# The two compressors' first layer as plain fp32 products of raw weights, keys and values in two column halves

## The reference, cut to what matters

```python
def compress(z, pe, w1, w2):
    c = z.reshape(B, T // CMP_STRIDE, CMP_STRIDE, G, N)
    blk = jnp.concatenate([c[:, :-1], c[:, 1:]], axis=2) + pe[None, None, :, None, :]
    blk = blk.transpose(0, 3, 1, 2, 4).reshape(B, G, n_cmp, CMP_LEN * N)
    return jax.nn.gelu(blk @ w1) @ w2

k_cmp = compress(kc, pe_k, ck_w1, ck_w2)
v_cmp = compress(vc, pe_v, cv_w1, cv_w2)
```

## Time and profile before

| | |
|---|---|
| median of 3 runs | 970.83 us (970.83 to 971.23) |
| profiled execution | 971.14 us, of which span 969.3 us |
| TensorE busy | 949.5 us (98%), granted clock 0.999 |
| VectorE, ScalarE, GpSimd busy | 703.2, 422.5, 439.5 us |
| chain that ended last | TensorE 83%, VectorE 12% |
| `CLO` on GpSimd, `CHI` on ScalarE | eight each, median 2.41 and 1.06 us |

### The profile page before, as it was taken

How to read it: one execution, slowest core, us unless ns; L and a number is a source line. 1 busy time by engine, 2 the same in 40 slices (tenths; PEclk the granted TensorE clock), 3 DMA queues, 4 the chain that set the end, 5 groups by cost and what they waited for, 6 DMA issues and landing times.

```text
span 969.3 us, 20667 instructions
## 1 busy us (share of the span) xinstructions
PE 949.5 (98%) x8504; PEld 767.3 (79%) x8504; DVE 703.2 (73%) x1170; ACT 422.5 (44%) x846; POOL 439.5 (45%) x473
## 2 busy tenths in 40 slices
PE   7999999999999999999999999999999999999997
PEld 5788777777777777776777888888999888888886
DVE  3799797565655966869777870489787774489987
ACT  4134341323313525546574454553444443345573
POOL 3367547335442865767665466445223225500000
PEclk9999999999999999999999999999999999999999
DMA  9344633212222648525336548043333433345452
GB/s 259 103 131 133 139 87 69 43 35 70 77 59 65 195 131 186 153 67 130 59 100 176 148 150 263 24 152 109 89 111 112 118 96 87 97 142 177 138 194 89
DMA packets 157365, 115.47 MB, mean 119 GB/s; under 512 B 21413, under 2 KB 139951, under 8 KB 157272
## 3 DMA queue, kind: packets, MB, share of 16 engines
q1 hardware_dynamic: 147820, 105.21, 37.8%
q10 hardware_dynamic: 9420, 8.95, 4.0%
q0 software_dynamic: 32, 0.00, 0.0%
HBM read 102.84 MB, written 11.30 MB: 118 GB/s over the span
## 4 chain that ended last, share of the span: by engine, by line
PE 83%; DVE 12%; issue 2%; ACT 1%; DMA 1%; POOL 0%; SPq 0%; DVEq 0%; ACTq 0%
PE ps L2424 32%; PE ps L2903 5%; PE ps L2902 5%; PE ps L2907 5%; PE ps L2544 3%; PE ps L2790 3%; PE ps L2963 2%; PE ps L2964 2%; PE ps L2965 2%; PE ps L2733 2%; PE ps L2940 2%; PE ps L2937 2%; PE ps L2936 2%; DVE XF L1517 2%; PE ps L2438 1%
## 5 line engine op out<-in xcount | busy, mean ns | idle before, releaser
L2424 PE MATMUL ps<-HHI,WHI 128*128 128x512 f32 x440 | 176.8, 402 | 0.7 <-DVE HLO L1549 0.7
L2424 PE MATMUL ps<-HLO,WHI 128*128 128x512 f32 x440 | 176.8, 402 | 0.0
L829 POOL TENSOR_TENSOR WLO<-WRAW,WHI 128x1024 fp32r<-128x1024 f32 (+1 forms) x51 | 103.2, 2026 | 102.1 <-ACT WHI L949 102.0
L930 POOL TENSOR_TENSOR WLO<-WRAW,WHI 128x512 fp32r<-128x512 f32 x50 | 72.5, 1457 | 118.6 <-ACT WHI L1317 117.2
L2424 PE MATMUL ps<-HHI,WLO 128*128 128x512 f32 x440 | 117.6, 397 | 0.0
L870 POOL TENSOR_TENSOR WLO<-WRAW,WHI 128x256 fp32r<-128x256 f32 x136 | 108.7, 802 | 14.4 <-ACT WHI L1166 7.0
L2424 PEld LDWEIGHTS ps<-HHI,WHI 128*128 128x128 f32 x440 | 82.6, 188 | 24.9 <-issue 7.5
L2424 PEld LDWEIGHTS ps<-HLO,WHI 128*128 128x128 f32 x440 | 82.6, 188 | 19.2 <-issue 1.6
L2424 PEld LDWEIGHTS ps<-HHI,WLO 128*128 128x128 f32 x440 | 80.7, 188 | 18.4 <-issue 1.4
L833 POOL CAST WHI<-WRAW 128x256 fp32r<-128x256 f32 (+1 forms) x93 | 46.7, 503 | 100.4 <-PE ps L2424 100.2
L2903 PE MATMUL ps<-HLO,WHI 128*128 128x512 f32 x200 | 77.9, 389 | 0.0
(11 more groups left out here) (512 smaller groups left out, 2316.1 us busy)
## 6 DMA issues: line engine op xcount, KB each, us to landing
WRAW<-in_w_in SPq DMA_DIRECT2D x47, 512.0 KB, 4.5
WRAW<-in_w_gate SPq DMA_DIRECT2D x22, 512.0 KB, 3.8
WRAW<-in_w_up SPq DMA_DIRECT2D x22, 512.0 KB, 3.8
WRAW<-in_w_down SPq DMA_DIRECT2D x19, 512.0 KB, 3.5
spilled<-SQ SPq DMA_DIRECT2D x24, 256.0 KB, 2.5
GATES<-spilled SPq DMA_DIRECT2D x6, 768.0 KB, 5.0
WRAW<-in_w_in SPq DMA_DIRECT2D x16, 256.0 KB, 3.5
WRAW<-in_w_branch SPq DMA_DIRECT2D x32, 128.0 KB, 2.9
```

The source lines that it names most:

```text
L829: return pool.tensor_tensor(lo[:, 0:chunks, :], WRAW[:, n % NRAW, 0:chunks, :], hi[:, 0:chunks, :].bitcast(F32), ALU.subtract)
L930: pool.tensor_tensor(lo, raw_half(item[1], item[2]), hi.bitcast(F32), ALU.subtract).then_inc(w_lo, 1)
L2424: last = pe.matmul(DB[g % 2][:, :], (wlo if which == "low" else whi)[:, c, :], lo if which == "x_low" else hi, start=a == 0, stop=a == 3 * ...
```

## The change

The eight `cmp` jobs leave the list. SP loads the raw weights of a part for keys and for values into two pairs of own buffers `CRAW` (`cmp_weights`); parts 0 and 1 are loaded ahead of the tiles rwkv 6 and rwkv 7, parts 2 and 3 ahead of rwkv 11 and rwkv 12, when the products of part 0 and of part 1 are done. TensorE multiplies `XF` by `CRAW` as they are, in plain fp32, in four packs of eight products (`compressed`) behind the tiles rwkv 7, 8, 9 and 10. In a pack products for keys and for values alternate: the keys' 62 stationary columns lie in the lower half of the array's columns and write rows 0 to 61 of `R[4]`, the values' lie in the upper half and write rows 64 to 125 of the same columns. `CHI`, `CLO`, `XHI`, `XLO` and what made them are gone. `HG` becomes 128 x 256: VectorE clears it and copies the two halves, the gelu's operations run on 256 columns, and two transposes of 128 x 128 take the place of four of 62 x 128. ScalarE's squares of `KK` stand behind rwkv 9's rounding instead of the next job's. Two semaphores of other uses are merged into one (`preset_ok`).

```diff
-for _n in range(8):
-    JOBS.append(("cmp", _n // 4, _n % 4, 4))
-    JOBS += _rw(6 + _n)
+JOBS += _rw(*range(6, 14))
...
+CMP_AFTER = (7, 8, 9, 10)
+CMP_LOADS = [AT["rwkv", _n, 0] for _n in (6, 7, 11, 12)]
...
-    XLO = [at("XLO0", 96, [P, 16, 2 * NCMP], F32R), at("XLO1", 80, [P, 16, 2 * NCMP], F32R)]
-    CHI = at("CHI", 68, [P, 8, P], F32R)
-    CLO = at("CLO", 72, [P, 8, P], F32R)
+    CRAW = [[at(f"CRAW{s}{kv}", (68, 72, 76, 92)[2 * s + kv], [P, 4, CH]) for kv in range(2)] for s in range(2)]
...
-    HG = SSUM[0:2 * NCMP, :].rearrange("p (k n) -> p k n", k=2)
+    HG = SSUM[:, 0:CH]
...
+            def cmp_weights(part):
+
+                if part == 0:
+                    sp.wait_ge(xsq_ok, 2)
+                    sp.wait_ge(xsum_ok, 2)
+                    sp.wait_ge(xT_done, KC)
+                if part >= 2:
+                    sp.wait_ge(cmp_mm, part - 1)
+                for kv, w in enumerate((ck1, cv1)):
+                    sp.dma_start(CRAW[part % 2][kv][:, :, :], chunked(w[part * 4 * P:(part + 1) * 4 * P, :], 0, CH))\
+                        .then_inc(cmp_in[part % 2], 16)
+
             for n in range(FF0):
+                if n in CMP_LOADS:
+                    cmp_weights(CMP_LOADS.index(n))
...
-                if n == AT["rwkv", 4, 0]:
-                    x_high(0)
...
-                if n == AT["rwkv", 8, 0]:
-                    x_high(1)
-                if n == AT["rwkv", 9, 0] + 1:
+                if n == AT["rwkv", 9, 0]:
                     for m in range(4):
                         act.wait_ge(kk_raw, m + 1)
...
-                    if i == 5:
-                        compress_low(0)
...
-                if i == 8:
-                    compress_low(1)
...
-            dve.wait_ge(dense_done, CMPS[-1] + 1)
-            dve.tensor_copy(HG[:, :, :], R[4][0:2 * NCMP, :].rearrange("p (k n) -> p k n", k=2)).then_inc(cmp_read, 1)
+            link(dve.memset(HG[:, :], 0.0))
+            dve.wait_ge(cmp_mm, 4)
+            for kv in range(2):
+                rows = slice(64 * kv, 64 * kv + 2 * NCMP)
+                ins = dve.tensor_copy(HG[rows, :], R[4][rows, 0:CH])
+            ins.then_inc(cmp_read, 1)
...
-            def cmp_product(n, k, hi, lo, start, stop):
-
-                kv = JOBS[n][1]
-                dst, cols = R[4][0:2 * NCMP, CH * kv:CH * kv + CH], slice(2 * k, 2 * k + 2)
-                whi, wlo = (w[:, cols, :].rearrange("p k n -> p (k n)") for w in split_of(n))
-                pe.matmul(dst, hi, whi, start=start, stop=False)
-                pe.matmul(dst, lo, whi, start=False, stop=False)
-                return pe.matmul(dst, hi, wlo, start=False, stop=stop)
+            def compressed(part):
+
+                pe.wait_ge(cmp_in[part % 2], 32 * (part // 2 + 1))
+                if part == 0:
+                    pe.wait_ge(xf_ok, 8)
+                for c in range(4):
+                    for kv in range(2):
+                        last = pe.matmul(R[4][64 * kv:64 * kv + 2 * NCMP, 0:CH], XF[kv][:, 4 * part + c, :],
+                                         CRAW[part % 2][kv][:, c, :], start=part + c == 0, stop=part == 3 and c == 3,
+                                         skip_group_check=True)
+                last.then_inc(cmp_mm, 1)
...
-            upto(AT["rwkv", 10, 0] + 2)
+            for part, i in enumerate(CMP_AFTER):
+                upto(AT["rwkv", i, 0] + 1)
+                compressed(part)
...
-            for i in range(4):
-                last = tr(R[1][:, 64 * i:64 * i + 2 * NCMP], HG[:, i // 2, P * (i % 2):P * (i % 2) + P], 2 * NCMP)
+            for h in range(2):
+                last = tr(R[1][:, P * h:P * h + P], HG[:, P * h:P * h + P])
```

More of the change, by code:

```diff
@@ L214, in tile_done @@
     return ITEM[("half", n, 1)] + 1
-def is_cmp(n):
-    return JOBS[n][0] == "cmp"
 def group_of(n):
-    return sum(not is_cmp(m) for m in range(n))
-DENSE = [n for n in range(NJ) if not is_cmp(n)]
-CMPS = [n for n in range(NJ) if is_cmp(n)]
+    return n
 def slot_of(n):
-    return NSPL + 6 if is_cmp(n) else HOME.get(n, group_of(n) % NSPL)
+    return HOME.get(n, n % NSPL)
 def slot_free(n):
[L237 to L240, removed]
+    return FREE.get(n, n - NSPL + 1 if n >= NSPL else 0)
 def width_of(n):
-    return 8 if is_cmp(n) else JOBS[n][3]
+    return JOBS[n][3]
 def loaded_value(n):
@@ L661, in job_sources @@
         kind, i, part, _ = JOBS[n]
-        every, full = slice(0, P), slice(0, {"cmp": CH, "out": T}.get(kind, P))
+        every, full = slice(0, P), slice(0, T if kind == "out" else P)
         if kind in ("nsa", "swa") and i < 4:
@@ L698, in raw_of @@
         slot = WRAW[:, n % NRAW, 0:width_of(n), :]
-        wide = {"cmp": CH, "out": T}.get(JOBS[n][0])
-        return slot.rearrange("p k n -> p (k n)").rearrange("p (k n) -> p k n", n=wide) if wide else slot
+        return slot.rearrange("p k n -> p (k n)").rearrange("p (k n) -> p k n", n=T) if JOBS[n][0] == "out" else slot
     class Chain:
@@ L2361, in rhs @@
                 kind, i, part, _ = JOBS[n]
-                if kind == "cmp":
-                    kv, c = i, 4 * part + k
-                    return XHI[kv][:, c, :], XLO[kv][:, c, :]
                 if kind == "branch":
@@ L2400, in steps @@
                     if k == 0:
-                        pe.wait_ge(*((w_lo, n + 1) if kind == "cmp" else (w_hi, n + 1)))
-                        if g >= 2 and kind != "cmp":
+                        pe.wait_ge(w_hi, n + 1)
+                        if g >= 2:
                             pe.wait_ge(dense_evac, g - 1)
-                        if kind == "cmp":
-                            pe.wait_ge(xsplit_ok, i + 1)
                         if kind == "branch":
                             pe.wait_ge(olo_ok, 4 * (i % 3) + 4)
-                    if kind == "cmp":
-                        hi, lo = rhs(n, k)
-                        last = cmp_product(n, k, hi, lo, part == 0 and k == 0, part == 3 and k == 3)
-                    else:
-                        order = products_of(n)
-                        first_low = min(a for a, (which, _) in enumerate(order) if which == "low")
-                        whi, wlo = split_of(n)
-                        for a in range(3 * k, 3 * k + 3):
-                            which, c = order[a]
-                            hi, lo = rhs(n, c)
-                            if n == 0 and which == "x_low":
-                                pe.wait_ge(xlo_ok, c + 1)
-                            if n == 0 and which == "x_high":
-                                pe.wait_ge(*((xhigh_ok, c + 1) if c else (xlo_ok, 1)))
-                            if a == first_low:
-                                pe.wait_ge(w_lo, n + 1)
-                            last = pe.matmul(DB[g % 2][:, :], (wlo if which == "low" else whi)[:, c, :],
-                                             lo if which == "x_low" else hi, start=a == 0, stop=a == 3 * chunks - 1)
@@ new lines, in steps @@
+                    order = products_of(n)
+                    first_low = min(a for a, (which, _) in enumerate(order) if which == "low")
+                    whi, wlo = split_of(n)
+                    for a in range(3 * k, 3 * k + 3):
+                        which, c = order[a]
+                        hi, lo = rhs(n, c)
+                        if n == 0 and which == "x_low":
+                            pe.wait_ge(xlo_ok, c + 1)
+                        if n == 0 and which == "x_high":
+                            pe.wait_ge(*((xhigh_ok, c + 1) if c else (xlo_ok, 1)))
+                        if a == first_low:
+                            pe.wait_ge(w_lo, n + 1)
+                        last = pe.matmul(DB[g % 2][:, :], (wlo if which == "low" else whi)[:, c, :],
+                                         lo if which == "x_low" else hi, start=a == 0, stop=a == 3 * chunks - 1)
```

52 lines of the change are left out of this document (20 added, 32 removed).

## The result

The change takes **973.72 us** (median of 16 runs, 972.09 to 974.65) against 971.28 us for the kernel before, measured beside it (16 runs, 970.83 to 972.37): a ratio of 1.0021, 95% interval 1.0014 to 1.0028. It is slower, by 2.4 us, where 4.35 us less were forecast; the range ended at 969.7.

A forecast was written before the change was run, and what follows sets the result against it. TensorE was taken as the bound, VectorE close behind. Terms -11.2 - 0.4 + 6.9 + 1.35 + 0.2 - 0.8 - 0.4 = -4.35 us, off the median 970.83, gave 966.5 us; range 964.3 to 969.7.

The forecast's parts named there:

- eight `cmp` jobs: TensorE, behind dense tiles: jobs of 12 products, 1.40 us each, all on the path, go away; 11.2 us less.
- wait for `XLO`: TensorE, fifth `cmp` job: its standstill for the low part goes away; 0.4 us less.
- 32 pairs of records: TensorE, packs: fp32 records for keys and values run together in column halves, 0.215 us a pair; 6.9 us more.
- edges of four packs: TensorE, entering and leaving the alternating form: about 0.34 us per pack; 1.35 us more, lower bound nothing.
- wait for the last `XF`: TensorE, first pack: waits for the last `compress_in` behind tile rwkv 6; 0.2 us more, bounds 0 and 1.0.
- wait for `SQLO`: TensorE, sums of the key norms: the wait goes as VectorE is through earlier; 0.8 us less, bounds 0 and 0.8.
- wait for `gn_bonus`: TensorE, group norm: the wait on VectorE goes as gelu operations halve to 256 columns; 0.4 us less.
- two transposes for four: Two transposes of 128 rows in place of four of 62 come out even; 0 us.
- the column halves running serially: Rival at the packs: 256-column streams run one after the other, 6.9 us more, 973.4 us; chance 0.08.
- Weight loads: Rival at the packs: each of 32 pairs waits for a 0.133 us load, 4.3 us more, 970.8; chance 0.03.
- VectorE does not keep TensorE waiting: Denies a rival: last `compress_in` meets one more `WLO`, first pack waits 2.4 us, total 969.9; chance 0.09.
- fewer durations above 2 us: Sign on VectorE: with `CLO` gone from GpSimd, line 1555, successor of line 1573, has fewer operations above 2 us.

The follow-up runs named there:

- experiment 4: The change with 19 padding products, keys' and values' products both put in one column half: 977.59 us, 1.0057 of the kernel before.
- with 168: The change with 168 already met waits ahead of products of dense tiles 8 to 14: 967.28 us, 0.9959 of the kernel before.

## Why the prediction was wrong

**Its sum held.** Term by term, in the trace of the change:

| term | forecast us | measured us | how |
|---|---|---|---|
| eight `cmp` jobs | -11.2 | -11.2 | 1.40 less at each dense tile that had one behind it |
| wait for `XLO` | -0.4 | -0.4 | that tile's shift is +0.16 where its neighbours' is +0.56 |
| 32 pairs of records | +6.9 | +6.9 | 0.216 from pair to pair |
| edges of four packs | +1.35 | +1.3 | 1.97 per pack up to the dense product, 0.11 more at the second one in three of four, less 1.73 for the pairs |
| wait for the last `XF` | +0.2 | 0 | no idle time ahead of 72.66; `XF` was there some 0.15 before |
| wait for `SQLO` | -0.8 | -0.8 | 1.86 in place of 2.68 |
| wait for `gn_bonus` | -0.4 | -0.5 | shift at the group norm's first product |
| two transposes for four | 0 | -0.3 | shift at 365.50; two take 0.14 up to the next product, four took 0.39 |
| late code blocks | none | +0.5 | 0.6 gone at 256.48, 1.1 come at 291.82 |

By the product at 365.50 the change is 3.84 us ahead, 4.24 counted from the 0.40 by which this execution began later; the sum was 4.35. That the two totals are so near is in part luck: the last two rows, of which the prediction has the one at nothing and the other not at all, and shifts of 0.2 around 180 us nearly cancel the other differences. The kernel with the bias load moved ends 4.37 us before the kernel before in the profile, and its median of 966.78 lies 0.3 from the forecast of 966.5 (4.6 under the kernel before measured beside it). For the edges the prediction had a lower bound of nothing, as the `cmp` jobs show it, and took the rows that alternate, rightly.

**The step that failed** is this one: "What follows is the same program on a TensorE that comes earlier, with other overlaps of VectorE and GpSimd; for these I allow 0.6 either way." What follows was the same program, but not cut into code blocks at the same places. The change makes TensorE's program 75 instructions shorter, and the allowance of 0.6 stood where +6.7 came (from -3.84 to +2.82): 4.2 us for a code block behind a 1 MB load and 3.1 at the lower clock, less 0.5 for a wait for VectorE that a later TensorE no longer has. No rival named it; the slower side was given to the column halves running serially, which experiment 4 excludes, and 0.07 was too little for all that wasn't listed.

**What the profile of before had of it.** The page shows the same 67 packets of queue q8, and TensorE's timeline this row:

```profile
256.48 0.64 PE L2544 MATMUL ps<-XX,AM 64*64 64x64 f32 x29 [0.59 <-issue]
```

That idle time of 0.59 us is the same thing: it begins behind record 5,313, which is 20 x 256 + 193. All stalls of this kind in the thirteen other traces stand at the 193rd to 195th of 256: 6,850 and 10,433 in the change, 7,105 and 10,690 in the kernel before with 180 waits, 10,689 with 168. A list of the boundaries 75 instructions later, beside the timeline, would have shown one in the group of products behind the bias load, with 4.4 us from boundary to boundary (440.72 to 445.08 in the kernel before). Among products as short as these, the blocks of the change that no burst holds up land mostly 1.4 to 3.7 us after the boundary at which they are asked for, and in all fourteen traces TensorE goes on 1.2 us after the landing at the earliest.

**The other rivals.** Weight loads do not come to light: pairs stand 0.216 us apart. VectorE does not keep TensorE waiting: no idle time at the first pack or at the sums, though at the pack it was close. GpSimd has no `CLO`, but the sign "fewer durations above 2 us" was wrong: of the 14 operations of line 1555 nine are above 2 us, beside `WLO` now, against seven of line 1573 (median 2.6 and 1.8). The waits that the sign was meant to show are gone all the same.

## What to carry to other kernels

An edit that changes the number of an engine's instructions moves every later boundary between its code blocks; look for "issue" idle time in the middle of a row of like products, count instructions modulo 256, and check what the DMA queues carry when a block of short products runs. Where a block holds short products, keep large transfers that nobody needs soon out of the way of the next one: here a block of 4.4 us was too short for a fetch that took 7.2 us behind a 1 MB load, and that load, wanted 25 us after it landed, cost 7 us. And a small difference between two versions says little on an edit until both have their stalls of this kind taken out; two versions may be compared with a few met waits as padding, put where the products hide them.

## What the runs showed that was not expected

- A block of TensorE's code that is asked for in a burst waited for 6 us: the boundary ahead of it is passed at 436.89, its packet moves at 443.16, is through at 444.13, and TensorE goes on at 445.56. With the burst moved, the packet moves 0.6 us after the boundary (436.52, 437.11).
- One such stall of 3.96 us costs nearly twice its length: the granted clock falls to 0.50 behind it, and 3.07 us more are lost. Behind stalls of 0.9 us the granted clock stays at 1.00.
- Waits that are met cost nothing among dense products (72 of them, under 0.05 us per tile), while 38 records of 32x32 products at the start put off the transposes behind them by 2.18 us, 0.06 each, and the first dense product by 3.13.
- Streams of 256 columns run beside each other in the two column halves without loss: 0.216 us for a pair of fp32 records, as for one alone in experiment 4.
